# The state-space core takes its heads' running sums from memory by a transfer per step instead of from a matmul

## The reference

```python
adt = dt * a                                  # (chunk, group, head, token)
a_cs = cumsum(adt, over tokens of a chunk)
decay = exp(where(tril, a_cs[l] - a_cs[s], -inf))      # 128 x 128 for each head
cb = einsum('bclgn,bcsgn->bcgls', C, B)                # 128 x 128 for each group
y_diag = einsum('bcgls,bcghls,bcsghp->bclghp', cb, decay, x * dt)
states = einsum(B, exp(a_cs[-1] - a_cs), x * dt)       # carried to the next chunk
y_off = einsum(C, previous state, exp(a_cs))
y = y_diag + y_off + D * x, gated by silu(z), normed by group
```

## Time and profile before

| | us |
|---|---|
| runs | 2231.19, 2232.34, 2235.20 (median 2232.34) |
| the profiled execution | 2231.84 |
| its span | 2230.0 |
| PE busy, of the span | 2098.9 (94%) |
| DVE busy | 1004.9 (45%) |
| ACT busy | 720.6 (32%) |
| POOL busy | 245.0 (11%) |
| chain that ended last | PE 73%, DMA 12%, DVE 8%, ACT 4% |

### The profile page before, as it was taken

How to read it: one execution, slowest core, us unless ns; L and a number is a source line. 1 busy time by engine, 2 the same in 40 slices (tenths; PEclk the granted TensorE clock), 3 DMA queues, 4 the chain that set the end, 5 groups by cost and what they waited for, 6 DMA issues and landing times.

```text
span 2230.0 us, 31114 instructions
## 1 busy us (share of the span) xinstructions
PE 2098.9 (94%) x13432; PEld 1476.9 (66%) x13432; DVE 1004.9 (45%) x1653; ACT 720.6 (32%) x1081; POOL 245.0 (11%) x218
## 2 busy tenths in 40 slices
PE   5999999999999898999999988997899989999998
PEld 3845744444443696444444438975899989998997
DVE  3434511111111564111111108865579846777983
ACT  3234211111111442111111118855455534444552
POOL 0000000000000000000000000056126400003540
PEclk9999899999999999999999999999999999999999
DMA  9777699999999557999999985422345554434552
GB/s 325 253 272 281 245 414 421 421 421 421 421 421 419 189 205 327 422 421 421 421 421 421 421 344 191 163 102 76 114 154 187 189 191 114 114 114 151 190 171 94
DMA packets 216208, 616.86 MB, mean 277 GB/s; under 512 B 20224, under 2 KB 107392, under 8 KB 166656
## 3 DMA queue, kind: packets, MB, share of 16 engines
q1 hardware_dynamic: 208960, 612.01, 71.5%
q10 hardware_dynamic: 7104, 2.76, 0.5%
HBM read 613.69 MB, written 1.05 MB: 276 GB/s over the span
## 4 chain that ended last, share of the span: by engine, by line
PE 73%; DMA 12%; DVE 8%; ACT 4%; POOL 1%; SPq 1%; issue 1%; ACTq 0%; DVEq 0%; POOLq 0%
PE bank L587 26%; PE bank L1331 16%; DMA ring<-in_moe_w_up 10%; PE bank L1340 7%; PE bank L1350 4%; PE bank L575 3%; PE bank L1310 3%; DVE ring_rounded L303 3%; PE bank L571 2%; ACT ring_rounded L297 2%; PE bank L374 2%; DVE arena L2480 1%; DMA ring<-in_mla_w_dq 1%; PE bank L621 1%; PE bank L622 1%
## 5 line engine op out<-in xcount | busy, mean ns | idle before, releaser
L1331 PE MATMUL bank<-ring,arena 128*64 128x512 f32 x2048 | 454.2, 593 | 12.0 <-DMA ring<-in_moe_w_up 12.0
L587 PE MATMUL bank<-normed_rounded,ring_rounded 128*128 128x256 f32 x3424 | 415.4, 283 | 4.9 <-ACT normed_rounded L683 3.4
L587 PEld LDWEIGHTS bank<-normed_rounded,ring_rounded 128*128 128x128 f32 x3424 | 411.1, 189 | 6.9 <-issue 4.3
L1331 PEld LDWEIGHTS bank<-ring,arena 128*64 128x64 f32 x2048 | 149.2, 137 | 305.3 <-issue 304.4
L1672 DVE TENSOR_TENSOR arena<-arena,bank 64x512 f32<-64x512 f32 x64 | 43.6, 681 | 658.7 <-ACT arena L1494 658.7
L303 DVE TENSOR_TENSOR ring_rounded<-ring,ring_rounded 128x4096 fp32r<-128x4096 f32 (+2 forms) x66 | 286.8, 4345 | 114.9 <-ACT ring_rounded L297 114.7
L587 PE MATMUL bank<-arena_rounded,ring_rounded 128*128 128x256 f32 x2336 | 290.9, 284 | 6.8 <-ACT arena_rounded L1923 2.6
L587 PEld LDWEIGHTS bank<-arena_rounded,ring_rounded 128*128 128x128 f32 x2336 | 283.3, 190 | 9.1 <-ACT arena_rounded L1923 3.4
L297 ACT ACTIVATE ring_rounded<-ring 128x4096 fp32r<-128x4096 f32 (+2 forms) x66 | 227.8, 3452 | 39.3 <-DMA ring<-in_ffn_w_down 31.4
L1340 PE MATMUL bank<-ring,arena 128*64 128x512 f32 x1024 | 233.9, 598 | 3.8 <-ACT arena L1501 3.8
L1494 ACT ACTIVATE arena<-bank 64x512 f32<-64x512 f32 x64 | 38.1, 596 | 441.7 <-PE bank L1331 441.7
(11 more groups left out here) (274 smaller groups left out, 2078.4 us busy)
## 6 DMA issues: line engine op xcount, KB each, us to landing
ring<-in_moe_w_gate SPq DMA_DIRECT2D x128, 1024.0 KB, 16.3
ring<-in_moe_w_up SPq DMA_DIRECT2D x128, 1024.0 KB, 18.5
ring<-in_moe_w_down SPq DMA_DIRECT2D x128, 1024.0 KB, 18.0
ring<-in_w_mod SPq DMA_DIRECT2D x24, 2048.0 KB, 11.4
ring<-in_ffn_w_up SPq DMA_DIRECT2D x44, 1024.0 KB, 7.1
ring<-in_ssm_w_in SPq DMA_DIRECT2D x12, 2048.0 KB, 8.0
ring<-in_ffn_w_down SPq DMA_DIRECT2D x10, 2048.0 KB, 8.0
ring<-in_conv_w_in SPq DMA_DIRECT2D x6, 2048.0 KB, 7.9
```

Of the source, the lines that this page charges most:

```text
L587: end = e.matmul(out, lhs.bitcast(F32R), rhs.bitcast(F32R), start=start and n == 0 and k == 0, stop=stop and n == 2 and k == n_k - 1)
L1331: ends[i] = e.matmul(bank[rows, :], xt[:, n * KD // 2 + j, :], weights[:, j, :], start=n == 0 and j == 0, stop=n == 1 and j == KD // 2 - 1)
```

## The change

The running sums are no longer spread by the matmul of ones. `sums_tensor` makes them once as rows (32 heads on partitions, 128 tokens of each chunk in columns) in one bank; ACT copies them to SBUF at m == 22 of the convolution phase and stores them in memory at m == 23. For each step a transfer, issued by ACT, reads the four heads' rows and spreads them over 128 partitions into one of four buffers E (two are the former ramp buffers, two lie in the arena): 1 KB to each partition in each of two halves, 256 KB in all. The transfers of steps 0 to 2 are issued ahead of `activate(30)`, the one of step s + 3 at the end of ACT's iteration s. The decay (DVE) and its exponential (ACT) are made two steps ahead, in place in E. The ramp (POOL) and the decay matmul with its bank (PE) are gone.

```diff
-        self.R, self.E = [idle(0), idle(1)], [ar.take(HG, P), ar.take(HG, P)]
+        self.E = [view.rearrange("p m (h t) -> p m h t", h=2) for view in (idle(0), ar.take(2, 2 * P), idle(1), ar.take(2, 2 * P))]
+        self.rows = k.nc.dram_tensor("ssm_sum_rows", [NC, HEADS, P], F32, kind="Internal").ap()
...
         # sums_tensor
+        bank, emptied = k.banks.next(k.act, "ssm sum rows")
+        w.wait_ge(*emptied)
+        for c in range(self.NC):
+            end = e.matmul(bank[0:HEADS, c * P:(c + 1) * P], self.adt[:, c, :], k.mat("upto"), start=True, stop=True)
+        end.then_inc(*k.pe.up("ssm sum rows"))
...
         # scores_tensor
-        bank, emptied = k.banks.next(k.dve, "decay", s)
-        w.wait_ge(*emptied)
-        w.wait_ge(*k.pool.at("ramp", s))
-        e.matmul(bank[:, :], k.mat("ones"), self.R[s % 2], start=True, stop=True).then_inc(*k.pe.up("decay", s))
...
         # scalar
+            if m == 22:
+                w.wait_ge(*pe.at("ssm sum rows"))
+                e.activation(self.by_heads[0:HEADS, :], banks.of("ssm sum rows")[0:HEADS, 0:T], ACT.Copy
+                             ).then_inc(*act.up("ssm sum rows"))
+            if m == 23:
+                w.wait_ge(*act.at("ssm sum rows"))
+                e.dma_start(self.rows.rearrange("c h t -> h c t"), self.by_heads[0:HEADS, :].rearrange("h (c t) -> h c t", c=NC)
+                            ).then_inc(*self.rows_stored.up("rows"))
...
+        def rows_of_step(s):
+            grp, c = divmod(s, NC)
+            if s >= 4:
+                w.wait_ge(*pe.at("diag", s - 4))
+            source = self.rows[c:c + 1, grp * HG:(grp + 1) * HG, :].rearrange("c (m h) t -> c m (h t)", m=2)
+            e.dma_start(self.E[s % 4].rearrange("p m h t -> p m (h t)"), source.broadcast_to([P, 2, 2 * P])
+                        ).then_inc(*self.rows_landed[s % 4].up(s))
+        w.wait_ge(*self.rows_stored.at("rows"))
+        for s in range(3):
+            rows_of_step(s)
         activate(30)
...
-            w.wait_ge(*dve.at("decay", s))
-            e.activation(self.E[s % 2], self.E[s % 2], ACT.Exp).then_inc(*act.up("decay", s))
+        def decays(s):
+            w.wait_ge(*dve.at("decay", s))
+            e.activation(self.E[s % 4], self.E[s % 4], ACT.Exp).then_inc(*act.up("decay", s))
...
+        decays(0)
         scores(0)
+        decays(1)
         for s in range(self.steps):
             if s + 1 < self.steps:
                 scores(s + 1)
+            if s + 2 < self.steps:
+                decays(s + 2)
...
+            if s + 3 < self.steps:
+                rows_of_step(s + 3)
...
         # vector
         def decay(s):
-            if s >= 2:
-                w.wait_ge(*pe.at("diag", s - 2))
-            w.wait_ge(*pe.at("decay", s))
+            w.wait_ge(*self.rows_landed[s % 4].at(s))
             w.wait_ge(*dve.at("ssm sums"))
             for h in range(HG):
-                end = e.tensor_scalar(self.E[s % 2][:, h, :], banks.of("decay", s)[:, h * P:(h + 1) * P],
-                                      acs[:, c, head:head + 1], 0.0, ALU.subtract, ALU.min)
+                row, head = self.E[s % 4][:, h // 2, h % 2, :], grp * HG + h
+                end = e.tensor_scalar(row, row, acs[:, c, head:head + 1], 0.0, ALU.subtract, ALU.min)
...
         decay(0)
+        decay(1)
         weigh(0)
         for s in range(self.steps):
-            if s + 1 < self.steps:
-                decay(s + 1)
+            if s + 2 < self.steps:
+                decay(s + 2)
             add(s)
...
         # gpsimd
-        ramp(0)
-        ramp(1)
...
-            if s + 2 < self.steps:
-                ramp(s + 2)
```

More of the change, by code:

```diff
@@ L2011, in __init__ @@
         halves = lambda m: k.X[:, m, SEQ:].rearrange("p (a t) -> p a t", a=2)
-        self.R, self.E = [idle(0), idle(1)], [ar.take(HG, P), ar.take(HG, P)]
+        self.E = [view.rearrange("p m (h t) -> p m h t", h=2) for view in (idle(0), ar.take(2, 2 * P), idle(1), ar.take(2, 2 * P))]
+        self.rows = k.nc.dram_tensor("ssm_sum_rows", [NC, HEADS, P], F32, kind="Internal").ap()
+        self.rows_stored = k.counted("ssm_rows_stored", 16)
+        self.rows_landed = [k.counted(f"ssm_rows_landed_{i}", 16) for i in range(4)]
         self.CB, self.CB_masked = ([halves(m)[:, n, :] for n in range(2)] for m in (4, 5))
@@ L2153, in sums_of_step_tensor @@
             m, cols = h // 2, slice(h % 2 * HEAD_P, (h % 2 + 1) * HEAD_P)
-            end = e.matmul(bank[:, h * HEAD_P:(h + 1) * HEAD_P], self.E[s % 2][:, h, :],
+            end = e.matmul(bank[:, h * HEAD_P:(h + 1) * HEAD_P], self.E[s % 4][:, m, h % 2, :],
                            self.XC[s % 2][:, m, cols], start=True, stop=True)
@@ L2495, in decay @@
             grp, c = divmod(s, NC)
-            if s >= 2:
-                w.wait_ge(*pe.at("diag", s - 2))
-            w.wait_ge(*pe.at("decay", s))
+            w.wait_ge(*self.rows_landed[s % 4].at(s))
             w.wait_ge(*dve.at("ssm sums"))
             for h in range(HG):
-                head = grp * HG + h
-                end = e.tensor_scalar(self.E[s % 2][:, h, :], banks.of("decay", s)[:, h * P:(h + 1) * P],
-                                      acs[:, c, head:head + 1], 0.0, ALU.subtract, ALU.min)
+                row, head = self.E[s % 4][:, h // 2, h % 2, :], grp * HG + h
+                end = e.tensor_scalar(row, row, acs[:, c, head:head + 1], 0.0, ALU.subtract, ALU.min)
             end.then_inc(*dve.up("decay", s))
         def weigh(s):
-            e4 = self.E[s % 2]
+            e4 = self.E[s % 4]
             w.wait_ge(*act.at("decay", s))
             w.wait_ge(*pool.at("masked", s))
-            e.tensor_tensor(e4, e4, across(self.CB_masked[s % 2], HG), ALU.mult).then_inc(*dve.up("weighted", s))
+            e.tensor_tensor(e4, e4, across(across(self.CB_masked[s % 2], 2), 2), ALU.mult).then_inc(*dve.up("weighted", s))
         def add(s):
@@ L2582, in gpsimd @@
         upto = k.mat("upto")
[L2584 to L2590, removed]
         def values(s):
```

## The result

| | before | after |
|---|---|---|
| median of the runs, us | 2233.05 (2231.19 to 2235.20, 4 runs) | 2248.21 (2245.21 to 2248.64, 4 runs) |
| ratio to before, 95% interval | | 1.0065 [1.0053, 1.0077] |
| profiled execution, us | 2231.84 | 2245.21 |
| its span, us | 2230.0 | 2243.2 |

The change makes the kernel 0.65% slower. The forecast was 2231, no change, with a range to 2246: wrong in its value, and just outside the range.

The account below looks back on a forecast made before the run. The prediction took a ring through ACT, DMA and DVE, not PE, as the bound; issue times summed through the steps ended 1.9 us earlier, 0.4 was given back for POOL, nothing counted outside: median 2231, range 2221 to 2246.

Parts of the forecast that it names:

- The count of the banks: In the steps: z(4) waits for the first quarter's Silu, PE standing some 11 us; holes of 3.85 and 3.84 go.
- The ring through ACT: Rows 3 to 15: ACT's issue, transfer, DVE's decay, exponential, rounding, next issue; 5.04 us a turn, 5.34 in even steps.
- The 14 us of removed matmuls: In PE's 16 steps: 0.86 less each, buying little, as a plain step stays about 5.19.
- The low clock at the turnings: Iteration 8, after 5 us of standing: PE turns in 1.96 and needs 1.68 for diag.
- Outside the steps I count nothing: Two small matmuls, a copy and an issue lie under waits of ACT; without that cover they cost 1.0.
- The first diag at 66.25, 0.5 later: Opening of the steps: the first diag comes 0.5 later, rows 0 to 2 leaving beside a weight transfer.
- L: Transfer's issue to landing in the ring: 2.7, bounds 2.2 and 4.0, with 1.0 added for rows 6, 9, 13.
- a sign of being wrong: Landings under 2.3 or over 3.2; PE without holes in steps 1 to 3; a hole at another step.
- in full by decay, exponential, rounding quarter and only then the next issue: From iteration 1 on, ACT issues the next transfer only behind these; rounding to the next counts 0.95 a turn.
- So the ring and not PE is the bound: In the steps: a turn takes 5.04 or 5.34, against PE's step of 4.33.
- Collisions with POOL, 0.4: In the steps: 0.4 us given back for decays that meet POOL's scale.
- the third rival: POOL holds DVE's decays, 0.5 at each of 13: 6.5 less 0.4, giving 2237; chance 7%.

Follow-up runs that it names:

- j: Changed kernel, each step's transfer bringing only the first of its two halves, 128 KB in place of 256: 2245.34, ratio 1.0062 to the kernel before.
- a: Changed kernel, rows of sums made in columns 256 to 511 of the column sums' bank, without a bank of their own: 2244.32, ratio 1.0045.
- d: Kernel before, with only the making and storing of the rows added, which nothing reads: 2240.24, ratio 1.0025.
- b: Changed kernel, transfers of steps 0 to 2 issued earlier, at m == 25 of the convolution phase: 2242.32, ratio 1.0038.
- c: Changed kernel, the transfer of step s + 3 issued ahead of the exponential of step s + 2: 2242.82, ratio 1.0038.
- i: Changed kernel, each of DVE's decays made over 127 of its 128 columns: 2246.52, ratio 1.0061.
- g: Kernel before, with ACT's rounding moved ahead of its quarter work (z, square, root or high): 2232.57, ratio 0.9993.
- k: Kernel before, ACT's rounding ahead of its quarter work and finished z banks dealt again behind the diag and state matmuls: 2232.76, ratio 0.9999.
- l: Kernel before, rounding first, z banks dealt again behind diag and state matmuls, POOL's ramp ahead of mask and values: 2221.33, ratio 0.9943.
- e: Changed kernel, the two banks of a finished z quarter dropped behind the z matmuls instead of ahead: 2239.25, ratio 1.0026.
- f: Changed kernel with four edits: rows in the sums' bank, first transfers at m == 25, transfers ahead of exponentials, z banks dropped late: 2228.87, ratio 0.9980.
- h: Changed kernel with the four edits of f and ACT's rounding ahead of its quarter work: 2218.72, ratio 0.9933.

## Why the prediction was wrong

By its own steps. Its sum for the profiled execution was 2230.3; measured 2245.21, so 14.9 us are missing.

**What held.** The count of the banks: z(4) stood 11.35 us for Silu where I had some 11, and no stand came at steps 8 and 12, where 3.85 and 3.84 had been. The ring through ACT up to step 4: the issues of rows 3 to 6 lie 15.0 us apart where I had 15.4, and Silu comes behind them. The 14 us of removed matmuls bought little. The low clock at the turnings: 1.75 and 1.81 where I had 1.96 and 1.68. This is the kernel after at step 7, behind a stand of 4.84 for POOL's scale:

```profile
1525.56 1.75 PE L575 MATMUL bank<-mats_rounded,arena 128*128 128x128 f32 x7 [0.52 <-POOL arena L2441]
1527.11 1.81 PE L2158 MATMUL bank<-residual,arena 128*128 128x64 f32 x8
```

**"Outside the steps I count nothing".** The first step that failed. I priced the instructions (1.0 uncovered) and not the bank. I had written that the extra bank shifts the deal and followed the shift only into the steps; ahead of them it moves PE's wait for VectorE one tile earlier in PE's program, while VectorE empties the bank no earlier. PE stood 1.4 longer, and the fall of its clock cost about 1.5 more: in j the stand is the same 2.94, the clock in the window 1438.5 to 1440 stayed at 1.00, and the stretch between the two turnings took 38.3 in place of 39.8. The last turning ahead of the steps came 4.2 later: 2.9 from stand and clock, 0.7 from the two small matmuls, and 0.6 that is there already at 1407, ahead of the change's first instruction, and is scatter. a and d show it from both sides: 1.0065 to 1.0045 without the bank, 1.0 to 1.0025 with nothing but it.

**"The first diag at 66.25, 0.5 later".** The second step that failed. 73.47 was measured: the 4.2 above and 3.5 from the transfers. I saw the weight transfer beside them and put the whole opening at 0.5; against a transfer alone these took 4 to 5.5 longer each. b removes most of it.

**L: 2.7 alone, 3.7 beside weights.** The third, a term sized too small. It was 3.0 to 3.4 alone (over 3.2 I had named as a sign of being wrong), 5.5 and 6.6 beside (rows 9 and 6). Row 6 alone lengthened the stand of z(4) by 3.4 (c). I had interpolated between 128 KB and a full queue of small loads; no row showed a small transfer behind a large one, and the bounds should have been open to that side. The rule in the Trainium skill (DMA: Bandwidth & Descriptors, Queues, rings and completion order) is that a DMA engine takes turns between its queues packet by packet. By that a small transfer would be slowed by a large one on another queue and not shut out. The trace agrees for rows 0 and 9, which landed 2.4 and 5.6 us ahead of the weight transfer beside them; row 6 and row 2 landed 0.2 and 0.4 behind theirs, and for these it does not tell the two apart.

**The issue, "in full by decay, exponential, rounding quarter and only then the next issue".** Half wrong, to the kernel's favour: ACT's issue left at the start of the exponential ahead of the rounding in the program (the kernel after, timeline):

```profile
1480.63 0.63 ACT L2361 ACTIVATE arena<-arena 128x512 f32<-128x512 f32 x1 [3.50 <-DVE arena L2531]
1480.63 0.37 ACTq L2341 DMA_DIRECT2D residual<-ssm_sum_rows  x1
1481.16 1.04 ACT L312 ACTIVATE ring_rounded<-ring 128x1024 fp32r<-128x1024 f32 x1
```

So a turn was shorter by the 1.0 of the rounding. The first took 4.2 (issues at 1476.41 and 1480.63), the next two 5.6 and 5.2 with longer landings and held decays, 15.0 for three where I had 15.4.

**"So the ring and not PE is the bound".** True only up to Silu at z(4). PE, up to two steps behind the decays, ran steps 1 to 3 at its own 4.34 without a hole (diag matmuls at 1480.21, 1484.56 and 1488.90), which I had named as a sign of being wrong. DVE waited for a transfer nine times and not thirteen, and 11.3 of the 15.2 us lie up to row 6. From the issue of row 7 to that of row 15 it took 59.0 us where I had 59.9, but there the number is right by luck: c issued each transfer ahead of the exponential and left four steps at 30.4, and in the chain of the changed kernel no landing stands behind row 6 (in those of a and b some do, so the two paths are nearly equal). What stands there from step 8 to 12 is ACT's rounding, DVE's rest and decay, POOL's scale and the turning of y.

**Collisions with POOL, 0.4.** Too small. The decays took 22.5 us for 64, against 17.8 before; by 0.87 for a free four it would have been 13.9. The long ones lie in the quarters, on the ring: 2.00 and 2.70 for rows 5 and 13, 1.81 for 11 and 15. L320, with two inputs in SBUF, was held too (2.19 in place of 1.23 at 1569.13, beside a mask of POOL's that took 1.44). A decay took 0.22 where it was free and 0.35 on average, where I had 0.19. Here the third rival was partly right. The rule of the Trainium skill that the prediction names (SBUF — State Buffer, Who interferes with whom) agrees with the pair of rows under i. Why 127 columns leave it so is open.

**The sum by terms,** in us later than forecast: 7.6 up to the issue of row 3 (0.6 scatter, 3.6 bank and small matmuls, 3.4 transfers); 0.4 less to that of row 6; 2.7 more to that of row 7, by row 6's landing; 0.9 less from there to the issue of row 15; 3.4 at the end (DVE's rest and decay held by POOL, and the last issue 1.0 nearer to its exponential than in my order); and 2.7 behind the steps. There the same 72 matmuls took 10.26 before and now 11.52, and the granted clock was 0.75 in place of 0.86 (windows of 12.23 us from their start):

```profile
1588.31 11.52 PE L2208 MATMUL bank<-arena_rounded,ring_rounded 128*128 128x256 f32 x72 [2.55 <-ACT arena L2366]
```

The other 1.4 lie spread over 640 us that the change does not touch. These terms make 15.1; less the 0.4 that the forecast had given back for POOL, and with 0.2 around the span, they are the 14.9. It was not shown why in the kernel after, with its Silu holes gone, 8 to 12 takes as long as before. That nearly equal waits lie behind one another is shown for both kernels: in the one before, g and k gained nothing and l brought four steps from 31.0 to 25.4; in the changed one, c left them at 30.4, e and f took 29.1, and only h, with the rounding first, 24.6.

## What to carry to other kernels

Where buffers are dealt in turn, an added user is priced by who then waits for whom, over the whole stretch that deals from the ring and not only around the edit. A stand that goes uncovers the next of nearly the same length: k removed two of 3.96 and gained nothing, until l cut the two of 5.21 behind them to 1.58. So before an engine's work is taken away for speed, try the order of the queues and of the banks, which here gave 0.57% without the change and, together with it, 0.67%. A small transfer on the path is priced beside the largest that can be issued ahead of it.

## What the runs showed of the hardware

- ACT's issue of a transfer leaves ahead of an activation that stands in front of it in the program, if both wait for nothing: issue at 1480.63, rounding 1481.16 to 1482.20. That transfer was not paced by the activation in front of it.
- A spread of 1 KB pieces to 128 partitions: 256 KB land in 3.0 to 3.4 us, 128 KB in 2.8 to 3.1. Up to 2.3 us behind a 2 MB weight transfer on SP's queue, or in the same moment, the same 256 KB take 5.5 to 8.8 in the changed kernel.
- Four tensor_scalars of 128 columns from SBUF: 0.87 us free, 1.2 to 2.7 beside POOL; from PSUM 1.09 to 1.13 for all 48 fours of before, k and l, with POOL or without. The form that is cheaper when free became the dearer one on average (22.5 against 17.8 for 64).
- After a stand of 2.93 us PE's granted clock was 0.50, the lower of its two levels, from 1438.50 to 1440.00 in the changed kernel, and 1.00 behind a stand of 1.55 in the kernel before. In j it was 1.00 behind a stand of 2.94, and the same 192 matmuls took 23.04 us in place of 24.57.
